# Expert weights in transfers of two units, with the down weights' rows dealt to partitions in fours

## The reference, cut to what matters

```python
def hier_moe(h, wg, bg, we, be, w_gate, w_up, w_down):
    ...
    gates = jax.nn.softmax(top_v, axis=-1) * pg
    ids = (g_sel * EXPERTS_PER_GROUP + top_i).reshape(-1).astype(jnp.int32)
    order = jnp.argsort(ids)
    tok = order // TOP_K
    xs = xf[tok]
    sizes = jnp.bincount(ids, length=N_EXPERTS).astype(jnp.int32)
    hg = lax.ragged_dot(xs, w_gate.astype(xs.dtype), sizes)
    hu = lax.ragged_dot(xs, w_up.astype(xs.dtype), sizes)
    ys = lax.ragged_dot(jax.nn.silu(hg) * hu, w_down.astype(xs.dtype), sizes)
    ys = ys * gates.reshape(-1)[order][:, None].astype(ys.dtype)
    y = jax.ops.segment_sum(ys, tok, num_segments=t)
```

## Time and profile before

| what | value |
| --- | --- |
| median of 3 runs | 3894.72 us (3892.78 to 3898.18) |
| the profiled execution, its own time | 3907.89 us |
| its span, first to last instruction | 3906.2 us |
| mean granted clock of PE over the span | 0.923 |
| busy share of the span: PE, DVE, ACT | 88%, 49%, 35% |
| moved by DMA | 442.90 MB, 113 GB/s over the span |
| 40th parts 35 to 39 of the span (in the expert stage) | 384 to 389 GB/s |

### The profile page before, as it was taken

One profiled execution on the slowest core, in us unless ns is written; L12 is line 12 of the kernel. 1 busy time (PEld: TensorE's weight loads), 2 busy tenths in 40 slices (PEclk: granted clock), 3 DMA queues, 4 the chain that ended last, 5 costly groups with the idle time before them and its releaser, 6 DMA issues. The chain is left out here.

```text
span 3906.2 us, 40359 instructions
## 1 busy us (share of the span) xinstructions
PE 3419.6 (88%) x15444; PEld 2793.8 (72%) x15444; DVE 1901.8 (49%) x2157; ACT 1370.0 (35%) x1947; POOL 182.0 (5%) x256
## 2 busy tenths in 40 slices
PE   6999999798899999995778879898978768999994
PEld 5888788686788888874567657687876546777773
DVE  3444335333344555545144740253332358888885
ACT  4323332213211111115122531123551326777783
POOL 0000000000000000000001100000000010000001
PEclk9999999898999999997888989898668888999997
DMA  3122221522111111102022021210002328999996
GB/s 93 60 87 77 71 65 54 189 86 86 60 49 49 48 48 48 40 14 93 1 49 97 28 70 44 60 48 22 22 11 86 108 83 315 387 386 389 384 384 244
DMA packets 302555, 442.90 MB, mean 113 GB/s; under 512 B 38769, under 2 KB 211313, under 8 KB 302449
## 3 DMA queue, kind: packets, MB, share of 16 engines
q1 hardware_dynamic: 277088, 353.30, 26.4%
q0 software_dynamic: 20752, 71.39, 5.1%
q10 hardware_dynamic: 4608, 16.78, 1.1%
HBM read 379.02 MB, written 62.39 MB: 113 GB/s over the span
## 5 line engine op out<-in xcount | busy, mean ns | idle before, releaser
L944 DVE TENSOR_TENSOR x_rows<-x_rows,ff_psd 128x512 f32<-128x512 f32 x352 | 239.5, 688 | 334.4 <-PE ff_psd L342 334.4
L340 PE MATMUL m_ps<-h_hl,m_w_hl 128*128 128x512 f32 x896 | 356.2, 398 | 11.8 <-DVE m_w_hl L527 11.8
L341 PE MATMUL m_ps<-h_hl,m_w_hl 128*128 128x512 f32 x896 | 349.8, 390 | 0.0
L342 PE MATMUL m_ps<-h_hl,m_w_hl 128*128 128x512 f32 x896 | 349.7, 390 | 0.0
L2351 DVE TENSOR_TENSOR h_hl<-ex_stage,h_hl 128x1024 fp32r<-128x1024 f32 x256 | 305.1, 1221 | 40.7 <-ACT h_hl L2347 40.3
L2347 ACT ACTIVATE h_hl<-ex_stage 128x1024 fp32r<-128x1024 f32 x256 | 269.0, 1058 | 83.3 <-DMA ex_stage<-in_exp_w_up_dram 47.8
L340 PEld LDWEIGHTS m_ps<-h_hl,m_w_hl 128*128 128x128 f32 x896 | 168.8, 188 | 50.7 <-DVE m_w_hl L527 12.1
L341 PEld LDWEIGHTS m_ps<-h_hl,m_w_hl 128*128 128x128 f32 x896 | 168.8, 188 | 38.6 <-issue 3.8
L342 PEld LDWEIGHTS m_ps<-h_hl,m_w_hl 128*128 128x128 f32 x896 | 168.7, 188 | 35.3
L924 ACT ACTIVATE ff_act_hl<-ff_act 128x1024 fp32r<-128x1024 f32 x22 | 23.3, 1061 | 485.3 <-DVE ff_act L962 485.3
L2351 DVE TENSOR_TENSOR ex_w_hl<-ex_stage,ex_w_hl 128x1024 fp32r<-128x1024 f32 x128 | 154.2, 1222 | 51.4 <-ACT ex_w_hl L2347 50.8
(11 more groups left out here) (528 smaller groups left out, 8004.8 us busy)
## 6 DMA issues: line engine op xcount, KB each, us to landing
ex_stage<-in_exp_w_gate_dram SPq DMA_DIRECT2D x128, 512.0 KB, 5.5
ex_stage<-in_exp_w_up_dram SPq DMA_DIRECT2D x128, 512.0 KB, 8.0
ex_stage<-in_exp_w_down_dram SPq DMA_DIRECT2D x128, 512.0 KB, 6.3
m_stage<-in_w_in_dram SPq DMA_DIRECT2D x56, 512.0 KB, 4.3
scratch_ys<-ex_ys ACTq DMA_DIRECT2D x32, 512.0 KB, 7.7
ff_stage<-in_w_ffn_gate_dram SPq DMA_DIRECT2D x22, 512.0 KB, 4.5
ff_stage<-in_w_ffn_up_dram SPq DMA_DIRECT2D x22, 512.0 KB, 5.8
ff_stage<-in_w_ffn_down_dram SPq DMA_DIRECT2D x22, 512.0 KB, 3.4
```

Of the source, the lines that this page charges most:

```text
L340: nc.tensor.matmul(out, w_hl[0], x_hl[0], start=first, stop=False)
L341: nc.tensor.matmul(out, w_hl[0], x_hl[1], start=False, stop=False)
L342: return nc.tensor.matmul(out, w_hl[1], x_hl[0], start=False, stop=last)
L944: v.tensor_tensor(dst, dst, ps_d[g % NB][:], ALU.add).then_inc(s_add, 1)
```

## The change

Two neighbouring units now travel in one transfer of 1 MB, into two neighbouring slots; each partition's part is a run of 8 KB in memory. To make that possible for the down weights, partition p holds the rows 4p to 4p+3 of the down matrix, so that unit k has row 4p+k on partition p. The product silu x up is therefore written in another order: column k*128+q of `act_f` comes from column 4q+k of the product. The six slot semaphores become three, one for a pair of slots; SP waits for the low parts of both units that were in the pair. Conversion on ACT and DVE and the products on PE go unit by unit, as before. In `further_tiles` the units stay single, and the product is written in the new order as well.

```diff
--- before.py
+++ after.py
@@ -2255,7 +2255,25 @@
     if u < 8:
         w = (A.exp_w_gate_2 if u < 4 else A.exp_w_up_2)[0].rearrange("e (p k) n -> e p k n", p=P)
         return w[e][:, 2 * (u % 4):2 * (u % 4) + 2]
-    return A.exp_w_down_2[0].rearrange("e (k p) n -> e p k n", p=P)[e][:, u - 8]
+    return A.exp_w_down_2[0].rearrange("e (p k) n -> e p k n", p=P)[e][:, u - 8]
+
+
+def weight_pair(A, u, e):
+
+    if u < 8:
+        w = (A.exp_w_gate_2 if u < 4 else A.exp_w_up_2)[0].rearrange("e (p k) n -> e p (k n)", p=P)
+        return w[e][:, 1024 * (u % 4):1024 * (u % 4) + 2048]
+    return A.exp_w_down_2[0].rearrange("e (p k) n -> e p (k n)", p=P)[e][:, 1024 * (u - 8):1024 * (u - 8) + 2048]
+
+
+def by_down_row(ap):
+
+    return ap.rearrange("p (q k) -> p q k", k=4)
+
+
+def turned_down_row(ap):
+
+    return ap.rearrange("p (k q) -> p q k", k=4)
 
 
 class Room:
@@ -2312,7 +2330,7 @@
     stage, w_hl, xg, xs_hl = mem.stage, mem.w_hl, mem.xg, mem.xs_hl
     silu, act_f, a_hl, ys, ident = mem.silu, mem.act_f, mem.a_hl, mem.ys, mem.ident
     ps_g, ps_u, ps_a, ps_d, ps_x = mem.ps_g, mem.ps_u, mem.ps_a, mem.ps_d, mem.ps_x
-    s_w, s_row, s_st = c.sems("ex_w_loaded", NS), c.sems("ex_rows_gathered", 2), c.sems("ex_ys_stored", 2)
+    s_w, s_row, s_st = c.sems("ex_w_loaded", NS // 2), c.sems("ex_rows_gathered", 2), c.sems("ex_ys_stored", 2)
     s_hi, s_lo, s_use = c.sem("ex_w_high"), c.sem("ex_w_low"), c.sem("ex_w_used")
     s_xt, s_xh, s_xl = c.sem("ex_rows_turned"), c.sem("ex_x_high"), c.sem("ex_x_low")
     s_silu, s_act, s_at, s_ah, s_al = (c.sem(f"ex_{n}") for n in ("silu_ready", "act_ready", "act_turned", "act_high", "act_low"))
@@ -2342,7 +2360,7 @@
 
     def high(act, e, u):
         s = slot(e, u)
-        act.wait_ge(s_w[s], loads(e, u))
+        act.wait_ge(s_w[s // 2], loads(e, u))
         wait(act, s_use, used_before(e, u))
         nc.scalar.activation(w_hl[u][:, 0], stage[:, s], ACT.Copy).then_inc(s_hi, 1)
 
@@ -2354,12 +2372,12 @@
 
         @block.sync
         def _(sp):
-            for at, u in in_order:
+            for at, u in in_order[::2]:
                 e = at - 1 if u >= 8 else at
                 n = number(e, u)
-                wait(sp, s_lo, n - NS + 1)
-                dst = stage[:, n % NS]
-                sp.dma_start(dst if u >= 8 else dst.rearrange("p (k n) -> p k n", n=F), weight_unit(A, u, e)).then_inc(s_w[n % NS], 16)
+                wait(sp, s_lo, n - NS + 2)
+                dst = stage[:, n % NS:n % NS + 2].rearrange("p a n -> p (a n)")
+                sp.dma_start(dst, weight_pair(A, u, e)).then_inc(s_w[n % NS // 2], 16)
 
         @block.scalar
         def _(act):
@@ -2481,7 +2499,7 @@
                     dve.wait_ge(s_silu, e + 1)
                     dve.wait_ge(s_use, number(e, 7) + 1)
                     wait(dve, s_at, e)
-                    v.tensor_tensor(act_f[:], silu[:], ps_u[:], ALU.mult).then_inc(s_act, 1)
+                    v.tensor_tensor(turned_down_row(act_f[:]), by_down_row(silu[:]), by_down_row(ps_u[:]), ALU.mult).then_inc(s_act, 1)
                     for u in range(8, 12):
                         low(dve, e, u)
 
```

## The result

The four runs of the changed kernel have a median of 3986.75 us (3978.39 to 3989.99), those of the kernel before beside them 3896.45 (3892.78 to 3901.23). The ratio is 1.0228, with a 95% interval of 1.0208 to 1.0248. The forecast was 3925 us with a range up to 3962. The sign was right; the loss is three times the 30 us that I worked out. The profiled execution took 3988.31 us.

What follows compares the result with a forecast made beforehand. Waits for late weights were taken to bound the expert stage, DMA engines or slots undecided; after the change, slot-pair rounds. 3907.9 + 28 (30 experts) + 2 (first expert) + 0 (product) = 3938 us profiled, 13 lower as median: 3925, range 3886 to 3962.

Steps and rivals of the forecast that it cites:

- Rounds of slot pairs bind: Expert stage: two rounds of three slot pairs set the step, 20.0 us an expert against 19.08; chance 0.67.
- The signs named for it: Expert stage: DMA share under 1.00, PE's wait near 2 us, ACT waiting only at first units, landings 6 to 7 us.
- issue to landing: Slot-pair round, weight transfers: least single landing plus the second unit's packets, 5.0 to 5.9 us.
- the 1.3 us for the gather and the row store: Expert's slot-pair rounds: one of these two transfers on the same engines delays a pair, 1.3 us, bounds 0 to 2.6.
- The 2 us for the first expert: First expert, where PE waits 3.86 us for ex_act: later landing and slot return add 2 us.
- Today the slots have slack: Expert stage before the change: six single slots need 16.3 us an expert at most, well under 19.08.
- a threshold of 8.5 us a round: Slot-pair rounds: staying under 8.5 us with collisions hidden would mean the pairs cost nothing.
- The first rival: Expert stage: DMA engines stay the bound, pairs cost nothing, longer runs gain 13 us, 3882 us; chance 0.16.
- The second rival: Expert stage: rounds come to 19 us, as if a 1 us term were hidden, 3895 us; chance 0.11.
- The third rival: Expert stage: rounds near 22 us, long PE waits lower its clock, 3985 us and up; chance 0.06.
- The product's form: DVE's silu times up, written with 512 B stride: 0.68 us plus at most 0.16, cost taken as 0.
- The 8 KB runs: Weight transfers on the DMA engines: 311 to 331 ns a run, saving 0.4 us an expert, at most 1.4.

Runs made afterwards that it cites:

- experiment 5: Kernel before with SyncE's refill and ACT's start both waiting for pairs, still single 512 KB transfers, old rows and product: 3981.9 us, ratio 1.0225.
- experiment 8: Changed kernel with four slot pairs in place of three, dealt rows, product written in order and read with a stride: 3893.43 us, ratio 0.9994.
- experiment 9: Changed kernel with four slot pairs in place of three, down rows and product as before the change: 3874.86 us, ratio 0.9947.
- experiment 7: Kernel before with eight single slots in place of six: 3866.94 us, ratio 0.9927.
- experiments 11 and 12: Changed kernel with 12, then 6, unused transposes on PE ahead of its wait for ex_act: 3978.82 us and 3980.2 us, ratios 1.0212 and 1.0208.
- experiment 10: Kernel before with eight single slots, down rows dealt in fours and product written with a stride: 3866.41 us, ratio 0.9925.
- experiment 3: Kernel before with SyncE's wait alone in pairs, then two single 512 KB transfers issued: 3933.43 us, ratio 1.0079.

## Why the prediction went wrong where it did

**The sign and the mechanism held.** Rounds of slot pairs bind: experiment 5 makes the loss with the waits alone, experiments 8 and 9 take it back with a fourth pair. What was wrong is the size of one term of the sum. The signs named for it came as well: share below 1.00, ACT's waits longer and only at the first unit of a pair, PE's wait 2.6 us an expert (2 forecast). The range ended at 3962 because I held the size for surer than it was.

**The term that failed is issue to landing, forecast at 5.0 to 5.9 us.** I took the least landings of one unit, 3.8 and 4.7 us, and added the second unit's packets. The least came out close to that, 4.9 us. But the median is 7.1: 2 x (7.1 + 3.5), and 0.3 us a round for the rest, are 21.8 us, the measured expert. The 0.3 is what is left over, not a measured duration. With the 1.3 us for the gather and the row store counted to the landings, the forecast had 2 x 5.45 + 1.3 = 12.2 us of landing in an expert; the trace has 14.2. These 2.0 us, 30 times, are 60 us, which is nearly the whole distance from 3925 to 3987. I had argued that landings would be "near their least time" once slots and not engines bind. They aren't. A pair is issued every 3.6 us and lands after 7.1, so two are under way on average, and the engines are still 92% busy. The waiting in the queue is a part of the round, not slack in it. The median before would not have given the right number either: 6.9 us and 1.2 for the second unit are 8.1, 1.0 too much, some 60 us in the time. How to get 7.1 from the rows before stays open; across these runs the median landing moved between 5.5 and 8.3 us. By tensor, the up pairs land after 8.0 us, the down pairs after 6.9, the gate pairs after 6.3:

```profile
ex_stage<-in_exp_w_up_dram SPq DMA_DIRECT2D x46, 1024.0 KB, 8.0
ex_stage<-in_exp_w_down_dram SPq DMA_DIRECT2D x46, 1024.0 KB, 6.9
ex_stage<-in_exp_w_gate_dram SPq DMA_DIRECT2D x45, 1024.0 KB, 6.3
```

**The 2 us for the first expert** did not come. From the first transfer of gate weights to the first product of silu and up it is 73.5 us before and 73.4 after; PE's wait there grew from 3.86 to 4.22 us.

**The same error stood in "Today the slots have slack".** I put the six single slots at 16.3 us at most with the least landings. With the median of the earlier trace rows, 6.9 us, two rounds are 2 x (6.9 + 1.06 + 1.22) = 18.4 us, and with the hand-overs nearly the 19.08 of the earlier trace rows. That this sum closes doesn't prove that slots bind. SyncE waits for all but every slot, so a slot's time must be 6 of 12 parts of an expert, 9.5 us, whatever the bound is; were the DMA engines the bound, the landings would be long as well. But it does say that the only slack a slot could have is inside its landing, and experiment 7 shows that the slots bound all the same. Had that been seen, any change that holds a slot longer was to be priced from 19.08 us on, not from a threshold of 8.5 us a round.

**The first rival** (the DMA engines bind) rested on the share of 1.00. It falls: 397 and 409 GB/s pass with eight slots, 415 in both experiments up to 3750 us, while weights are being fetched.

**The second rival** (both balance at 19 us) needed a term that is hidden; the expert took 21.82 us. The runs were not cut into 4 KB pieces either, as the packets of the queue show.

**The third rival** named the time, 3985 us, by the right first half (rounds near 22 us, 3 us an expert) and a second half, the clock, that does occur and by the estimate of experiments 11 and 12 is worth some 12 us. In that sum, too, the 90 us came from the rounds alone. That the first half would come was given 0.06; it belonged in the forecast's own bounds, whose upper end of 22.4 us an expert contained it while the range in us did not.

**The product's form** was bounded by 0.68 and 0.84 us and took 1.05: outside. The row that I scaled from writes pieces of 128 neighbouring elements, and here no two written elements are neighbours. Taking 0 for its cost was wrong as well, since where PE waits for ex_act the product is on that path: 7 us with the rows at six single slots, some 18 (with the rows and the down runs) at four pairs, none at eight single slots, where PE doesn't wait.

**The 8 KB runs** were to save 0.4 us an expert, at 311 to 331 ns a run. They took 363 ns in the changed kernel, against 369 for two runs of 4 KB in experiment 5, and 336 in experiment 8, against 324 in experiment 7: next to no gain, and none in the time, since the DMA engines were not the bound. A rule of the Trainium skill, page DMA: Bandwidth & Descriptors, section Bandwidth, asks for transfers of at least 1 MiB for 75% of the peak. These runs speak against using it here: transfers of 512 KB moved 385 GB/s with six slots and 397 to 409 with eight, those of 1 MB in the same memory 336 with six slots' worth and 392 to 405 with eight. What counted was how soon a slot's memory could take the next transfer.

## What to carry to other kernels

Before joining transfers, write down where a slot's time goes: landing, conversion, waiting for the engine behind. If the issuing engine waits for every slot, the parts always add up to step x slots / transfers a step (9.5 us before, 10.9 after, 11.7 in experiment 7), so that they add up proves nothing; their sizes tell. Where the slot waits after its landing for another engine, that engine binds, as in experiment 7: 5.5 us of landing, 2.3 of conversion, and some 3.9 behind ACT, which itself waits for PE. Where all of it is landing and conversion, the ring of slots or the DMA engines bind, and the DMA share doesn't say which; a run with two more slots does. If it is the ring, anything that holds a slot longer costs time, and the median landing, not the least, is what a round pays. Transfers of twice the size in the same memory halve the number of transfers that can be under way; spend new memory on more slots first (two more single slots gave 28 us here, the best of the versions run, and joining their transfers took some 8 us of them back, at the edge of the noise). A product on the way to a waiting engine should be written and read in order, or the order should be changed where another engine has time.

## What the runs showed of the hardware that was not expected

- The 128x512 product of an SBUF and a PSUM tile takes 0.68 us in order, 1.04 to 1.10 us written with 512 B between elements, and 1.07 us read with 16 B between them and written in order. Either side with a stride costs about 0.4 us.
- A DMA share of 1.00 went with 385 GB/s before, 392 in experiment 8 and 405 in experiment 9, 1.01 with 409 in experiment 10, and 1.02 with 415 in experiment 7 up to 3750 us. The share alone does not tell a queue that is full from engines that carry all they can.
- After an idle time of 5.02 us PE's granted clock was 0.55 over the next 3.5 us, and its products were back at 0.23 us apart at the end of them. Where another engine's chain set the step, giving half of the lost clock back changed the time by 6 us of 3987, within the uncertainty.
- The mean time of a 4 KB run of the weights was 162 ns in experiment 7, 170 before and 184 in experiment 5, while the DMA share up to 3750 us was 1.02, 1.00 and 0.94. The less was under way, the longer a run took.
- SyncE's transfer takes 0.33 us to issue for 512 KB and for 1 MB alike. With the old down rows (two runs a partition, experiment 9) a down pair takes 0.38 us. Where two transfers are issued one behind the other (experiment 3), the median is 0.38 us too, and the longest 1.27.
